# Expert rows added into an output with spare rows, and the gate weights' low halves made by VectorE

## What is computed

```python
ga, gb, gc = jnp.split(jax.nn.sigmoid(h @ gate_w[l] + gate_b[l]), N_BRANCHES, axis=-1)
mixed = ga * (ya @ proj_a[l]) + gb * (yb @ proj_b[l]) + gc * (yc @ proj_c[l])
x = x + g1[:, None, :] * (mixed @ w_out[l])
h2 = modulate(rmsnorm(x, norm2_g[l]), sh2, sc2)
x = x + g2[:, None, :] * hier_moe(h2, ...)
# inside hier_moe, for each block of 128 (token, expert) slots of one expert:
y = (jax.nn.silu(xblk @ w1[e]) * (xblk @ w3[e])) @ w2[e]
out = zeros.at[buf_tok].add(y * buf_w[:, None])
```

## Time and profile before

| | us |
|---|---|
| median of 3 runs (lowest, highest) | 2867.02 (2862.5, 2869.83) |
| profiled execution, its own time | 2870.37 |
| its span, first to last instruction | 2868.5 |
| PE busy in the span | 2717.7 (95%) |
| DVE busy | 1959.8 (68%) |
| ACT busy | 1511.4 (53%) |
| POOL busy | 394.5 (14%) |

### The profile page before, as it was taken

How to read it: one execution, slowest core, us unless ns; L and a number is a source line. 1 busy time by engine, 2 the same in 40 slices (tenths; PEclk the granted TensorE clock), 3 DMA queues, 4 the chain that set the end, 5 groups by cost and what they waited for, 6 DMA issues and landing times. The chain is left out here.

```text
span 2868.5 us, 41607 instructions
## 1 busy us (share of the span) xinstructions
PE 2717.7 (95%) x13546; PEld 2186.5 (76%) x13547; DVE 1959.8 (68%) x3202; ACT 1511.4 (53%) x2409; POOL 394.5 (14%) x287
## 2 busy tenths in 40 slices
PE   6999999999999997999989999978999999999996
PEld 5777887787778785888767878857777777777774
DVE  6754765646565565754557653458999999999984
ACT  4414664656566663333334431225777777777763
POOL 2101220000000001111100001111222232222211
PEclk8999999999999998999999999988999999999998
DMA  6475324141313227211268984438989989777884
GB/s 243 144 256 191 110 103 168 37 152 35 129 60 129 71 95 252 77 58 57 67 238 330 352 305 169 175 132 306 330 279 316 372 299 300 256 232 231 289 268 122
DMA packets 287583, 554.79 MB, mean 193 GB/s; under 512 B 28748, under 2 KB 95564, under 8 KB 285144
## 3 DMA queue, kind: packets, MB, share of 16 engines
q1 hardware_dynamic: 269048, 492.06, 48.0%
q0 software_dynamic: 14400, 52.44, 7.4%
q10 hardware_dynamic: 4000, 8.53, 0.9%
HBM read 418.21 MB, written 143.15 MB: 196 GB/s over the span
## 5 line engine op out<-in xcount | busy, mean ns | idle before, releaser
L2765 DVE TENSOR_TENSOR moe_w_lo<-moe_W,moe_w_hi 128x1024 fp32r<-128x1024 f32 x384 | 452.4, 1220 | 16.9 <-ACT moe_w_hi L2685 16.2
L2685 ACT CAST moe_w_hi<-moe_W 128x1024 fp32r (+1 forms) x384 | 398.8, 1053 | 98.8 <-PE moe_yb L2629 31.5
L1667 PE MATMUL project_bank<-h_lo,w_hi 128*128 128x512 f32 x512 | 200.8, 392 | 0.0
L355 PE MATMUL att_bank<-h_hi,w_hi 128*128 128x512 f32 x384 | 168.5, 439 | 7.5 <-PEq L141 4.2
L448 ACT ACTIVATE att_S<-att_S,att_nm,q_scale 128x128 f32<-128x128 f32 (+15 forms) x128 | 165.8, 1297 | 4.5 <-DVE att_nm L565 4.0
L2601 PE MATMUL moe_h1b<-moe_w_hi,moe_xT_hi 128*128 128x512 f32 x384 | 156.4, 407 | 4.8 <-DVE moe_xT_lo L2781 4.8
L556 DVE TENSOR_SCALAR_CACHE_REDUCE att_S<-att_bank 128x512 f32<-128x512 f32 x192 | 122.3, 687 | 54.4 <-PE att_bank L322 54.4
L726 POOL TENSOR_TENSOR w_lo<-w_raw,w_hi 128x1024 fp32r<-128x1024 f32 x15 | 38.5, 2564 | 830.4 <-ACT w_hi L719 830.4
L2603 PE MATMUL moe_h1b<-moe_w_hi,moe_xT_lo 128*128 128x512 f32 x384 | 151.6, 395 | 0.0
L357 PE MATMUL att_bank<-h_hi,w_lo 128*128 128x512 f32 x384 | 151.5, 394 | 0.0
L356 PE MATMUL att_bank<-h_lo,w_hi 128*128 128x512 f32 x384 | 151.1, 394 | 0.0
(11 more groups left out here) (522 smaller groups left out, 7085.9 us busy)
## 6 DMA issues: line engine op xcount, KB each, us to landing
moe_W<-in_moe_w SPq DMA_DIRECT2D x96, 2048.0 KB
w_raw<-in_gate_w SPq DMA_DIRECT2D x48, 512.0 KB, 3.8
out_sg<-gateT SPq DMA_DIRECT2D x32, 768.0 KB, 6.6
gateT<-att_gates SPq DMA_DIRECT2D x48, 256.0 KB, 2.0
gateT<-gate_out SPq DMA_DIRECT2D x48, 256.0 KB, 2.1
early<-in_ada_w SPq DMA_DIRECT2D x8, 1024.0 KB, 12.8
project_spare<-in_x SPq DMA_DIRECT2D x16, 512.0 KB, 6.2
zT<-project_oz SPq DMA_DIRECT2D x32, 256.0 KB, 3.4
```

Of the source, the lines that this page charges most:

```text
L355: pe.matmul(bank[7][:], w_hi[b][:, k, :], h_hi[:, k, at], start=k == 0, stop=False)
L1667: pe.matmul(bank[n % 4][:], w_hi[b][:, k, :], low[:, k, at512(tb)], start=False, stop=False)
L2685: nc.scalar.copy(w_hi[:, slot(p, first), :], raw(at, p)).then_inc(q["w13_high"], 1)
L2765: nc.vector.tensor_tensor(w_lo[:, own, :], raw(at, p), w_hi[:, own, :].bitcast(F32), ALU.subtract).then_inc(q["w1_low" if p < 4 else "w3_l ...
```

## The change

1. The output tensor gets 128 spare rows (`(1, T + P, D)`, the host returns the first T), and `acc` is this tensor. The copy, `write_rows`, `place_own`, `y2` and the tables for slots without a token are gone; all blocks go through `place_y` and `add_rows`. `LAST` is 3. The loop now runs 45 turns.
2. In the last turn (`final`) ACT casts the last block's three weight pieces ahead of `place_h`, and DVE subtracts them ahead of `place_y` of the block before; they wait for the second product of the block before, piece by piece.
3. `lower` runs on DVE, at places written out by hand in both stages; POOL has no instruction left in them.
4. The expert block is made with `no_gpsimd_drain=True`: its final barrier has no DRAIN instruction on POOL. `Stage.end` uses a barrier of semaphores alone, without DRAIN on the five engines.

```diff
-        self.nc.all_engine_barrier()
+        self.nc.all_engine_barrier(sem_only=True)
...
-    def lower(self, pool, j):
-        pool.wait_ge(self.w_high, j + 1)
+    def lower(self, dve, j):
+        dve.wait_ge(self.w_high, j + 1)
...
-        self.nc.gpsimd.tensor_tensor(...)
+        self.nc.vector.tensor_tensor(...)
...
                     wider(A[:], u, 1)
+                    if c == 0:
+                        fill.lower(dve, 0)
                     if c == 1:
                         wider(B[:], A[:], 2)
                         wider(A[:], B[:], 4)
+                        fill.lower(dve, 1)
                         wider(B[:], A[:], 8, slice(64, P))
...
                     nc.vector.tensor_copy(first[:, c, 0:16], u[:, 0:16]).then_inc(pooled, 1)
+                fill.lower(dve, 2)
...
                     by_power(E[:], Et[:], prev, B1, B2, q["e_ready"])
                     if tn:
+                        fill.lower(dve, 3 * tn + 3)
...
                     nc.vector.tensor_copy(K[:, 0:P], bank[3][0:GU * 16, 0:P]).then_inc(q["k_copied"], 1)
+                    fill.lower(dve, 3 * tn + 4)
                     dve.wait_ge(q["k_summed"], tn + 1)
...
+                        if lv == 3:
+                            fill.lower(dve, 3 * tn + 5)
                 dve.wait_ge(q["r_ready"], GU * LEVELS * TURNS)
+                for j in (15, 16):
+                    fill.lower(dve, j)
...
-    NBK, LAST = NB_OUT, 4
+    NBK, LAST = NB_OUT, 3
...
-        with nc.Block() as block:
+        with nc.Block(no_gpsimd_drain=True) as block:
...
                     if final:
+                        e = expert(act, b)
+                        for k in range(P2):
+                            high_2(b, e, k, True)
+                        high_third(b)
                         place_h(b)
-                        high_third(b)
                         return
...
-                    if n == LAST - 2:
+                    if final:
                         hidden(b)
-                        place_own(b - 1, n)
+                        e = expert(dve, b)
+                        for k in range(P2):
+                            low_2(b, e, k)
+                        low_third(b)
+                        place_y(b - 1)
                         split_h(b)
-                        low_third(b)
                         return
...
                 for n in range(LAST):
-                    b = count + n
-                    if n < LAST - 3:
-                        gather(b + 3)
-                    write_rows(b, n)
+                    add_rows(count + n)
...
-    g["acc"] = nc.dram_tensor("acc", (T + P, D), F32, kind="Internal").ap()
+    g["acc"] = g["out"][0]
...
-    g["out"] = nc.dram_tensor("out", (1, T, D), F32, kind="ExternalOutput").ap()
+    g["out"] = nc.dram_tensor("out", (1, T + P, D), F32, kind="ExternalOutput").ap()
...
-    return r.results[0]["out"]
+    return r.results[0]["out"][:, :T]
```

More of the change, by code:

```diff
@@ L793, in _ @@
                 sp.wait_ge(y_stored, 256)
-            @block.gpsimd
-            def _(pool):
-                for j in range(3):
-                    fill.lower(pool, j)
             @block.tensor
@@ L983, in _ @@
                     sp.wait_ge(y_stored[b], 128)
-            @block.gpsimd
-            def _(pool):
-                for j in range(20):
-                    fill.lower(pool, j)
             @block.tensor
@@ L1345, in _ @@
                     nc.vector.tensor_tensor(y, y, b, ALU.mult).then_inc(q["gelued"], 1)
+                    if n == 4:
+                        fill.lower(dve, 18)
+                fill.lower(dve, 19)
                 def low(n):
@@ L2728, in _, with turn @@
                 high_13(1, at, e, range(R, P13))
-                def turn(b, last=False, final=False):
+                def turn(b, final=False):
                     e = expert(act, b - 1)
@@ L2753, in _ @@
                 for n in range(LAST - 1):
-                    turn(count + (n + 1), n == 0, n == LAST - 2)
-                e = expert(act, count + (LAST - 1))
-                for k in range(P2):
-                    high_2(count + (LAST - 1), e, k)
+                    turn(count + (n + 1), n == LAST - 2)
             @block.vector
@@ L2935, in _, with gather @@
                 for n in range(LAST - 1):
-                    turn(count + (n + 1), n)
-                e = expert(dve, count + (LAST - 1))
-                for k in range(P2):
-                    low_2(count + (LAST - 1), e, k)
-                place_own(count + (LAST - 1), LAST - 1)
+                    turn(count + (n + 1), n == LAST - 2)
+                place_y(count + (LAST - 1))
             @block.gpsimd
             def _(pool):
-                def gather(b, first=False, table=own_tok):
+                def gather(b, first=False):
                     if not first:
                         pool.wait_ge(q["x_turned"], b)
-                    nc.gpsimd.tensor_copy(idx[:], table[:, bass.ds(b, 1)]).then_inc(q["idx_copied"], 1)
+                    nc.gpsimd.tensor_copy(idx[:], slot_tok[:, bass.ds(b, 1)]).then_inc(q["idx_copied"], 1)
                     pool.wait_ge(q["idx_copied"], b + 1)
```

77 lines of the change are left out of this document (13 added, 64 removed).

## The result

| us | before | changed |
|---|---|---|
| median (lowest, highest) of 3 runs | 2867.02 (2862.5, 2869.83) | 2837.68 (2834.76, 2840.92) |
| again, in a later series (a0 below) | 2868.49, 9 runs | 2841.04, 4 runs |
| profiled execution, its own time | 2870.37 | 2834.76 |
| its span | 2868.5 | 2832.9 |

The ratio of the runs is 0.99 with an interval of 0.9873 to 0.9927, and 0.9891 (0.9871 to 0.9911) in the later series. The kernel became 29.3 us faster by the medians, 27.4 in the later series. The later series' 2841.04 lies inside the range; its gain is 5.8 us larger than forecast, against 7.7 in the first.

What follows compares the result with a forecast made beforehand. PE, busy 95% of the span, was taken as the bound, with DMA bounding the end. Experts 17.6, pooling 1.4, SSM 2.4 and barriers 0.2 summed to 21.6 us less: 2845.4 us against 2867.02, range 2838.5 to 2854.5.

Steps and rivals of the forecast that it cites:

- Turns 46 and 47: Expert loop: without the copy into the output, both turns take 18.07 us, 10.54 us gone from PE's path.
- the fourth rival: Turns 46 and 47: the last experts' weights hold the gather, so 10.5 us are not won; 2855.9 us, chance 0.03.
- The order of the chain at the end: Last turn: placing ends at 2829.0, add starts about 1.0 later, lands at 2838.9; y_free, not PE, releases the last placing.
- the signs that I named: At the end: last `place_y` idle some 8 us, released by the add; last add landing within 1 us of span's end.
- The price of the last two adds: End of expert stage: an add lands after 8.9 us, the median of 44 in the loop.
- the third rival: Last two adds: no weights load beside them, so 6.0 us each and the end 5.6 sooner; 2839.8 us, chance 0.08.
- The DRAIN: End of expert stage: POOL's DRAIN goes away, 5.05 of the stage's 17.6 us.
- the barriers: Six barriers lose their engines' DRAINs: 0.2 us estimated, between 0 and 0.6.
- The first rival: Program end: the DRAIN's work comes back behind the last instruction; 2850.1 us, chance 0.20.
- Pooling: Pooling stage: three POOL stalls gone, three DVE subtractions added, a 1.0 us wait for a cast; 1.4 us less, bounds 0 to 2.8.
- SSM: SSM turns: 7.4 us of stalls for R gone, less 4.0 of gaps and 1.0 behind the last turn; 2.4 us less.
- Slower: Expert loop: adds into the output take longer than into `acc`; 2883 us at 16.5 us an add, chance 0.02.

Runs made afterwards that it cites:

- a0: The changed kernel once more with no edit: 2841.04 us, ratio 0.9891.
- a3: The changed kernel with the fourth level's subtraction in an SSM turn moved between R and the additions: 2835.43 us, ratio 0.9882.
- b1: The changed kernel with two more loads of 2 MB into unread weight tiles, beside the last two adds: 2845.04 us, ratio 0.9913.
- c2: The kernel before with one edit, no DRAIN on POOL behind the expert block: 2868.48 us, ratio 1.0003.
- c3: The kernel before with both barrier edits, no DRAIN behind the expert block and semaphores alone in `Stage.end`: 2862.32 us, ratio 0.998.
- a1: The changed kernel with the plain barrier, and so POOL's DRAIN, back behind the expert block: 2842.24 us, ratio 0.9901.
- a2: The changed kernel with the `lower` subtractions on POOL again: 2844.19 us, ratio 0.9911.
- b2: The changed kernel with the old order of the last turn, casts and subtractions behind the placing of the block before: 2844.26 us, ratio 0.9912.
- b3: The changed kernel with the SSM subtraction moved behind R, the last product by column halves and two half-row adds: 2835.88 us, ratio 0.9882.

## Why the prediction missed

**Turns 46 and 47:** right. 10.54 us were forecast from two turns of 18.07, 10.54 came. The last experts' weights are still loaded in turn 46 (174 GB/s) and hold no gather, so the fourth rival is out. That it was the copy's traffic, and not ACT's wait for `acc_done` or the other order of these turns, fits the rows, but no run took the copy away alone.

**The order of the chain at the end:** right in its parts. PE's first h transpose stands 16.8 us behind the turn's start in both kernels, the placing ends 2.5 us behind it (2.3 forecast), the add starts 1.0 behind that, and y_free releases the last placing. This hangs on the clock: the add landed at 2823.02, the product had ended at 2822.67. Where the product ran at 0.78 (a3) it ended later than the add, and released the placing. Of the signs that I named, the placing's idle time was 6.8 us and not 8, and the last add landed 1.3 us before the span's end and not within 1.

**The price of the last two adds:** the step that failed. I took 8.9 us, the median of the 44 adds in the loop, for two adds with nothing loaded beside them. They took 6.1 each, 5.6 us less for the two. The placing before them ended 0.2 us later behind the turn's start than I had put it, and the stretch behind the last landing was longer by 0.7, so the stretch gave 11.8 us in place of 7.1: 4.7 of the 7.7 us by which the forecast missed. The row for it was in my hands: the gather of output rows at 2852.95, with nothing loaded beside it, had landed and let the next instruction start after 1.58 + 4.66 = 6.2 us, and 6.0 was the least of the loop's adds. I had this case as the third rival, with its reason and with 2839.8 us, and gave it 0.08: the nearest row by kind of instruction won over the nearest row by state of the DMA engines. b1 shows that the state decides.

**The DRAIN:** the right size (4.6 to 5.7 us against 5.05), for an incomplete reason. I credited it to the one edit of the block and put the barriers at 0.2 us. c2 and c3 show that the edit of `Stage.end` is needed for all of it. Apart from the DRAIN the barriers were right in size: from the last DRAIN of the block's barrier to the end of the second one the border at 1082 us took 0.93 us and takes 0.58, and the other four ahead of the last kept theirs within 0.04. The first rival, that its work returns behind the last instruction, is out: a1, c3 and the changed kernel have the same 1.8 us outside the span. The Trainium skill's barrier and reset of the rings behind a kernel (Runtime: NRT & Kernel Launch, section The launch sequence) may be there, but these runs show no part of it that a DRAIN inside shortens.

**Pooling:** mis-sized, 2.4 us by a2 against 1.4, and what the forecast missed here is the clock. Three stalls gone, 6.2, less three subtractions, 3.7: 2.5. I took off more, because DVE would wait for ACT's casts. In the changed kernel's profile the third cast ended at 1111.15, before DVE came at 1111.36, and no wait came. But the casts stand on ACT behind the results of PE's gate groups, and the first of these came 1.3 us earlier behind the stage's start: 0.3 by the shorter barrier, the rest by the clock, which over the first 10 us of the stage was 0.66 in the kernel before and 0.77 here. In a1, whose pooling stage has the same instructions, it was 0.66 again. The windows of the three:

```profile
1081.60:1091.60 10.00, 9.01 (x27) 7.23 (x28) 8.80 (x7) 1.49 (x2) 3.62 (x1) 0.66 0.79 265
```

```profile
1080.83:1090.83 10.00, 9.36 (x33) 7.59 (x34) 9.05 (x10) 1.74 (x2) 0.00 (x0) 0.77 0.81 275
```

```profile
1081.24:1091.24 10.00, 9.36 (x29) 7.46 (x29) 9.05 (x10) 1.74 (x2) 0.00 (x0) 0.66 0.82 278
```

and there the forecast wait of 1.0 us stands:

```profile
1102.94 1.23 DVE L726 TENSOR_TENSOR gw_lo<-w_raw,gw_hi 128x1024 fp32r<-128x1024 f32 x1 [1.17 <-ACT gw_hi L719]
```

a1's stage took 49.45 us, 1.6 less than a2's 51.0 and close to the 1.4 forecast, and b2 and b3, at 0.71, took 49.1 and 49.4; the runs from 0.75 up took 48.4 to 48.7. So the wait was rightly seen, and its price depends on the clock at the stage's start.

**SSM:** right in size. Four gaps of 0.9 us (1.0 forecast) for eight of 7.4 in all, and 1.0 us behind the last turn, as forecast: 7.4 - 3.5 - 1.0 = 2.9 against 2.4; a2 gives 2.5 by PE's idle time.

**The range:** it was too narrow on its low side. The sum with the measured terms is 10.5 + 11.8 + 2.4 + 2.9 = 27.6 us, between the 27.4 and 29.3 of the two series, which differ by less than single executions do. Two terms erred to the same side, and the rival that held the larger of them stood at the range's edge with its own scatter left out.

**Slower:** nothing of it. The loop's adds land after 8.8 us in the median, as before, with 10.9 as the longest.

## What to carry to other kernels

Take the price of a transfer from a row with the same load on the DMA engines, before one with the same instruction: the last transfers of a program run alone and are cheaper than the median of a loop. Where a wait is priced against an instant of another engine, look what sets that instant: here it was PE's pace, and the granted clock at the stage's start made the wait 1.2 us or nothing. Look also where a DMA's issue on POOL falls among DVE's instructions that read two SBUF tiles. And when a costly synchronizing instruction is taken out, look for the next of its kind: its price may wait there.

## What the runs showed of the hardware

- A DRAIN on POOL took 0.29, 4.48, 4.72 and 5.05 us behind 3, 93, 96 and 100 indirect DMAs, though all of these had landed; it is paid once, by the first DRAIN behind them. Whether it goes by their number or by the time since the last DRAIN is open.
- An indirect add of 512 KB took 6.1 us alone at a DMA share of 0.54, and 8.3 beside a load of 2 MB. One of 256 KB took 4.6 and 5.2. By the fit of the Trainium skill (DMA: Bandwidth & Descriptors, section Anatomy of one DMA), 2.0 us plus the bytes over 436e3 per us, these would be 3.2 and 2.6 us: the measured ones are about twice that, so the fit doesn't hold for adds to scattered rows. It does for the plain write of 512 KB to scattered rows in the kernel before (line L2991), which landed after 3.4 us:

```profile
DMA to landing us min/median/max: 3.4/3.4/3.4
```

- The issue of an indirect add on POOL took 1.6 us. Where a DVE subtraction of two SBUF tiles was already running, it took what was left of that and 1.48 us more: 2.25 to 2.60 us in 11 adds of the changed kernel.
- The projecting stage, the same in all these kernels, lasted 461 to 468 us from execution to execution. In the merge stage length less PE's busy time stayed within 19 to 22 us while the length went from 424.4 to 428.1; in the projecting stage it did not stay as close (31.6 to 37.1).
- The last product, 22 matmuls, took 6.1 us at a granted clock of 1.00, 7.7 at 0.78 and 8.1 at 0.73. The profiles know two levels of the granted clock, full (1.00) and half; a mean in between mixes them. Behind a wait of PE of 4.6 us the product never ran at full clock throughout (five profiles); behind one of 2.4 or 2.5 us it did in five profiles and had 0.78 to 0.80 in three.
